# One core, a decoder trunk with experts: the results of each small expert item are scattered by the next small item

## The reference

```
def moe_swiglu(h, router, w_gate, w_up, w_down):
    tok = h.reshape(B * S, D)
    logits = (tok @ router).astype(jnp.float32)
    top_v, top_i = lax.top_k(logits, TOP_K_EXPERTS)
    w = jax.nn.softmax(top_v, axis=-1)
    gates = jnp.sum(jax.nn.one_hot(top_i, N_EXPERTS) * w[..., None], axis=1)
    out = jnp.zeros_like(tok)
    for e in range(N_EXPERTS):
        out = out + gates[:, e:e + 1] * swiglu(tok, w_gate[e], w_up[e], w_down[e])
    return out
```

## Time and profile before

| | |
|---|---|
| median of 3 runs | 1305.22 us (1303.74 to 1307.96) |
| the profiled execution | 1304.98 us |
| its span, first to last instruction | 1303.2 us |
| mean granted TensorE clock | 0.99 |
| PE busy | 1242.6 us, 95% |
| DVE busy | 637.7 us, 49% |
| ACT busy | 568.5 us, 44% |
| POOL busy | 112.3 us, 9% |
| read from HBM | 422.23 MB |

### The profile page before, as it was taken

One profiled execution on the slowest core, in us unless ns is written; L12 is line 12 of the kernel. 1 busy time (PEld: TensorE's weight loads), 2 busy tenths in 40 slices (PEclk: granted clock), 3 DMA queues, 4 the chain that ended last, 5 costly groups with the idle time before them and its releaser, 6 DMA issues.

```text
span 1303.2 us, 18423 instructions
## 1 busy us (share of the span) xinstructions
PE 1242.6 (95%) x7254; PEld 880.2 (68%) x7254; DVE 637.7 (49%) x754; ACT 568.5 (44%) x871; POOL 112.3 (9%) x262
## 2 busy tenths in 40 slices
PE   9999999999999999899999989999989999998776
PEld 8988999999989833577853367774338777333222
DVE  6886755547755300588820078880028885000001
ACT  6665544435656300577720177761027775001002
POOL 1000000000000461100210100201010021001000
PEclk9999999999999899999999999999999999999999
DMA  9943554358432399999999999999999999999996
GB/s 332 356 152 115 184 195 162 130 174 279 171 143 78 129 401 418 404 415 415 408 369 415 417 408 415 421 383 391 416 409 412 414 416 359 417 419 402 415 416 256
DMA packets 116487, 424.47 MB, mean 326 GB/s; under 512 B 4625, under 2 KB 23218, under 8 KB 108594
## 3 DMA queue, kind: packets, MB, share of 16 engines
q1 hardware_dynamic: 116192, 422.75, 83.0%
q10 hardware_dynamic: 210, 0.54, 0.1%
HBM read 422.23 MB, written 1.05 MB: 325 GB/s over the span
## 4 chain that ended last, share of the span: by engine, by line
PE 79%; DMA 17%; DVE 2%; ACT 1%; issue 1%; SPq 0%; POOL 0%; POOLq 0%; ACTq 0%; DVEq 0%
DMA ring<-in_moe_w_down 8%; PE psA L1571 7%; PE psA L1573 7%; PE psA L1572 7%; PE psB L1571 7%; PE psB L1573 7%; PE psB L1572 7%; DMA ring<-in_moe_w_up 6%; PE psA L1955 5%; PE psB L1955 5%; PE psY L1571 5%; PE psY L1573 5%; PE psY L1572 5%; PE psY L1946 4%; DMA ring<-in_moe_w_gate 2%; PE psY L1719 1%
## 5 line engine op out<-in xcount | busy, mean ns | idle before, releaser
L1436 DVE TENSOR_TENSOR wlo<-ring,whi 128x2048 fp32r<-128x2048 f32 (+1 forms) x135 | 287.2, 2150 | 84.9 <-ACT whi L812 83.9
L812 ACT CAST whi<-ring 128x1024 fp32r<-128x1024 f32 x252 | 261.0, 1051 | 89.1 <-PE psA L1573 28.6
L1183 DVE TENSOR_TENSOR wlo<-ring,whi 128x1024 fp32r<-128x1024 f32 (+2 forms) x104 | 152.3, 1485 | 17.8 <-ACT whi L630 17.7
L630 ACT CAST whi<-ring 128x1024 fp32r<-128x1024 f32 (+1 forms) x134 | 133.4, 1023 | 59.3 <-PE psY L1573 28.2
L1946 PE MATMUL psY<-ring,squares_of 128*64 128x512 f32 x560 | 126.8, 596 | 7.3 <-DMA ring<-in_moe_w_down 7.1
L1515 DVE TENSOR_TENSOR hidT<-psB,hidT 128x512 f32<-128x512 f32 (+1 forms) x16 | 10.0, 625 | 243.4 <-PE psB L1955 177.4
L1955 PE MATMUL psB<-ring,resT 128*64 128x512 f32 x480 | 106.6, 594 | 8.9 <-DMA ring<-in_moe_w_up 8.8
L1955 PE MATMUL psA<-ring,resT 128*64 128x512 f32 x480 | 107.6, 596 | 5.6 <-DMA ring<-in_moe_w_gate 5.6
L1571 PE MATMUL psA<-xhi,whi 128*128 128x256 f32 x368 | 104.9, 285 | 2.6 <-DVE wlo L1183 1.2
L1571 PE MATMUL psB<-xhi,whi 128*128 128x256 f32 x368 | 106.4, 289 | 0.0
L1572 PE MATMUL psA<-xlo,whi 128*128 128x256 f32 x368 | 102.8, 279 | 0.0
(11 more groups left out here) (351 smaller groups left out, 2265.0 us busy)
## 6 DMA issues: line engine op xcount, KB each, us to landing
ring<-in_moe_w_gate SPq DMA_DIRECT2D x56, 2048.0 KB, 19.0
ring<-in_moe_w_up SPq DMA_DIRECT2D x56, 2048.0 KB, 20.4
ring<-in_moe_w_down SPq DMA_DIRECT2D x56, 2048.0 KB, 21.0
ring<-in_ffn_w_gate SPq DMA_DIRECT2D x5, 2048.0 KB, 9.1
ring<-in_ffn_w_up SPq DMA_DIRECT2D x5, 2048.0 KB, 7.9
ring<-in_ffn_w_down SPq DMA_DIRECT2D x5, 2048.0 KB, 8.0
ring<-in_moba_w_qkv SPq DMA_DIRECT2D x8, 1024.0 KB, 7.4
ring<-in_diff_w_qkv SPq DMA_DIRECT2D x6, 1024.0 KB, 12.2
```

The lines of the kernel that those rows point to most:

```text
L630: nc.scalar.copy(hi_of(m, size), part_of(ring, s, g, size)).then_inc(hi_done, size)
L812: nc.scalar.copy(hi_of(NG + m, 2), item_part(ring, j, g, 2)).then_inc(hi_done, 2)
L1183: nc.vector.tensor_tensor(part_of(wlo, s, g, size), part_of(ring, s, g, size), f(hi_of(m, size)), ALU.subtract).then_inc(lo_done, size)
L1436: nc.vector.tensor_tensor(item_part(wlo, j, g, step), item_part(ring, j, g, step), f(hi_of(NG + m, step)), ALU.subtract).then_inc(lo_done, ...
```

## The change

The big items scatter nothing. The small items 2, 4 and 6 scatter two results each: that of the small item two places ahead (parts 0, 1 ahead of slot gate 3, parts 2, 3 ahead of slot up 3) and then that of the big item just ahead (ahead of slots gate 5 and up 5). The result of a small item waits in its buffer through the big item. The loop (item 7) scatters as before, at gate 3 and gate 5. The waits on `scatter_mm` and `add_done` are counted anew with `scattered(i)`, and each pair of scatter matmuls now waits for the adds of the pair before it.

```diff
-    SCATTER_AT = {item_slot["gate", 3, 2, 0]: (0, 2), item_slot["gate", 5, 2, 0]: (2, 4)}
+    SPREAD_AT = item_slot["gate", 5, 2, 0]
+    SCATTER_AT = [item_slot[kind, c, 2, 0] for c in (3, 5) for kind in ("gate", "up")]
@@
+        def scatters(i):
+            if not isinstance(i, int) or i >= LAST:
+                return {SCATTER_AT[0]: (i - 1, 0, 2), SCATTER_AT[2]: (i - 1, 2, 4)}
+            if not i or i in BIG_AT:
+                return {}
+            return {SCATTER_AT[a]: (i - 2 + a // 2, a % 2 * 2, a % 2 * 2 + 2) for a in range(4)}
+
+        def scattered(i):
+            return 4 * (i - 1 if isinstance(i, int) and i in BIG_AT else i)
@@ ACT, result
-                if not isinstance(i, int) or i:
-                    act.wait_ge(scatter_mm, 4 * i)
+                if not isinstance(i, int) or i >= 2:
+                    act.wait_ge(scatter_mm, scattered(i))
@@ DVE, few_rows
-                    if n in (1, 2):
-                        add_rows(i - 1, 2 * n - 2, 2 * n)
+                    for at, what in scatters(i).items():
+                        if n in (1, 2) and (at < SPREAD_AT) == (n == 1):
+                            add_rows(*what)
@@ DVE, expert
-                    if j in SCATTER_AT:
-                        add_rows(i - 1, *SCATTER_AT[j])
@@ PE, gather_rows
-                    if not isinstance(i, int) or i >= 2:
-                        pe.wait_ge(add_done, 4 * (i - 1))
+                    if not isinstance(i, int) or i >= 3:
+                        pe.wait_ge(add_done, scattered(i - 1))
@@ PE, scatter
-                if first:
+                if first or not isinstance(i, int) or i:
                     pe.wait_ge(add_done, 4 * i + first)
@@ PE, expert
-                    if j in SCATTER_AT:
-                        scatter(i - 1, *SCATTER_AT[j])
@@ PE, few_rows
-                    if j in SCATTER_AT:
-                        if not isinstance(i, int) or i:
-                            scatter(i - 1, *SCATTER_AT[j])
-                        elif SCATTER_AT[j][0]:
-                            spread_T()
+                    if j in scatters(i):
+                        scatter(*scatters(i)[j])
+                    if isinstance(i, int) and i == 0 and j == SPREAD_AT:
+                        spread_T()
```

## The result

| | before | after |
|---|---|---|
| median of 6 runs each | 1305.33 us (1300.12 to 1307.96) | 1294.04 us (1291.71 to 1297.49) |
| profiled execution | 1304.98 us | 1297.49 us |
| its span | 1303.2 us | 1295.7 us |
| PE busy | 1242.6 us | 1240.2 us |
| POOL busy | 112.3 us | 100.5 us |

The ratio is 0.9921, 95% interval 0.9898 to 0.9943: faster by 10.3 us by the ratio, and 11.3 us between the medians. Between the two profiled executions lie only 7.5 us, near the forecast of 6.4. The rest of this text is about both differences: what the 7.5 us are, and where 3 to 4 more come from.

What follows compares the result with a forecast made beforehand. The prediction took a DMA weight stream with three PE-made gaps at the big items' ends as the bound. Removing 2.12 us from each of three big items, 6.4 us, gave 1304.98 - 6.4 = 1298.6 us; range 1295.5 to 1303.0.

Steps and rivals of the forecast that it cites:

- What bounds the kernel: Whole expert part: DMA stream at some 413 GB/s, with three PE-made gaps of 3.3 to 3.8 us, one per big item.
- The sum: Whole kernel: 1304.98 - 6.4 = 1298.6 us, with all other parts of the change taken as worth nothing.
- the term of the removed pairs: Big items, PE: two scatter pairs of 1.06 us removed from each of three items, all regained as DMA time, 6.4 us.
- rival 1: Heads of items 3 and 5: full clock comes back too, giving 1297.0 us, or 1295.8 with both items; chance 0.22.
- The base: Starting time: the profiled execution, 1304.98 us, lies 0.24 us below the median, so no correction.
- The small items: Items 2, 4, 6: added pairs at 1.2 us each, 2.4 us an item, covered by 6.3 and 5.33 us of PE idle time.
- DVE, POOL and the new waits: Moved adds, `spread` writes, selection and added waits in big and small items: all cost or gain nothing.
- POOL's chain: Selection for item 3, ended 7.4 us after the scatter; moves into item 2, some 28 us ahead of the gather; costs nothing.
- Rival 2: Gaps at the big items' ends: slowest of 16 DMA engines goes on as before, half regained, 1301.8 us; chance 0.12.
- rival 3: Whole kernel: no change, 1305.0 us, as the DMA stream is untouched and gaps are not PE's or reappear elsewhere; chance 0.09.

Runs made afterwards that it cites:

- e6: Kernel before, with each pair of scatter matmuls in the big items made twice: 1310.11 us, ratio 1.0028.
- e5: Kernel before, with 36 useless transposes in PE's idle time ahead of each big item: 1298.92 us, ratio 0.995.
- e4: Changed kernel, with 36 useless transposes in PE's idle time ahead of each big item: 1295.81 us.
- e9: Kernel before, with twelve useless transposes in PE's short waits of the routing: 1301.54 us, ratio 0.9983.
- e8: Changed kernel, with three useless 128-row matmuls ahead of each of four scatter slots in small items 2, 4 and 6: 1306.99 us.
- e12: Kernel before, with two useless pairs of 64-row matmuls in each of small items 2, 4, 6 and twelve transposes in the routing: 1301.70 us.
- e10: Changed kernel, with twelve useless transposes in PE's short waits of the routing: 1292.86 us, ratio 0.9911.
- e1: Changed kernel measured again, unedited: 1293.74 us, ratio 0.9924.
- e2: Changed kernel, with the older result's scatter in small items 2, 4 and 6 only 8 columns wide instead of 512: 1297.02 us.
- e7: e4 with twelve more useless transposes in PE's short waits of the routing: 1291.90 us, ratio 0.9895.

## Why the prediction was wrong, point by point

**What bounds the kernel: right.** Three gaps at the ends of the big items, each made by PE, a DMA stream at full rate elsewhere. The shorter the big item, the higher the rate in the three windows: from 341 GB/s in e6 over 354 before, 386 in e5 and 398 after to 407 in e4 (means; set by the ends of the big items, over 50 us, they are 379, 387, 401, 409 and 412).

**The sum: the term of the removed pairs was too small.** It stood at 3 x 2 x 1.06 = 6.4 us. The pair is worth 1.24 us (1.23 at gate 3), since the step from the turn to the pair (0.53 us) is longer than the step from the turn to the product (0.35 us): 7.4 us. I measured the pair from its own start and did not bound what its absence does to its neighbour. Measured from head to head: 7.7 and 7.8 us. What is over 7.4 is not shown apart; the clock is the likely part. Item 5 had 6.8 us at half clock in the profile before, 5.6 of it in work; after, the stretch is 3.4 us, and the item got 3.5 us shorter where items 1 and 3 got 2.5. That is part of rival 1, though hardly for its reason: idle time ahead of item 5 fell by 0.7 us only, and e9 shows both lengths at idle times of 5.0 to 5.1 us.

**The base: the step that failed most.** "It lies 0.24 us below the median, so no correction is made." The profiled execution had the routing at half clock, and the median lay beside it in the upper group; 1300.12 came only with the later executions. Over all runs the executions of the kernel before lie from 1299.4 to 1308.0, most of them below 1303 or above 1304.7; those of the changed kernel at 1291.7 to 1295.6 and at 1297.3 to 1297.5. The median before came from the upper group, that after from the lower: two executions of twelve of the changed kernel lie in its upper group, of the kernel before four of 6 in the result above. With the routing still the two medians are 8.7 us apart instead of 11.3. The term of the pairs at its measured 7.4 us would have given 1297.6 us, and even 8.7 us below the median of 1305.3 would be 1296.6, both inside the range. What put the result below 1295.5 are the other 2.6 us, by these runs most likely the draw of executions with and without half clock in the routing. My range had no term for this, although the three times shown spread over 4.2 us. Whether the change itself makes the lower group likelier is open: e4 and e8, which have it too, have four of 6 (1295.4 to 1296.3, the others at 1291) and eight of 12 (1305.9 to 1309.7, the others at 1302.7) in their upper groups, which speaks for chance. The profiles in the last paragraph on e9 to e12 leave the same question open for the heads of the big items.

**The small items: right in sign, too dear.** I had 2.4 us of added work and 3.9 and 2.9 us of idle time left; it is 4.48 and 4.67. The pairs cost 1.06 us each, not 1.2, and part of them went into waits inside the small item: in item 2 PE had waited 1.33 us for `w_down` and 0.61 us ahead of the gather, and after the change it waits for neither. The cover holds, and e8 shows where it ends. Predicted heads of items 3 and 5: 755.3 and 969.7; found: 754.16 and 969.15.

**DVE, POOL and the new waits: right.** No wait of PE for `spread` or for adds shows in the small items after, and the selection written in item 2 is in time. The 7.4 us that I took for POOL's chain from the earlier trace rows came to 3.5 us (698.99 to 702.45), since the same copy of `rel_now` and the selection behind it are shorter there. Before, in big item 1, and after, in small item 2:

```profile
619.45 2.25 POOL L1119 COPY rel_now<-rel 128x4 f32<-128x4 f32 x1
```

```profile
699.67 0.19 POOL L1130 COPY rel_now<-rel 128x4 f32<-128x4 f32 x1
700.10 2.35 POOL L1136 TENSOR_SCALAR equal<-slotno,rel_now 128x128 f32<-128x128 f32 x4
```

DVE was busy for 7.33 of 9 us around the first (618 to 627) and for 1.13 of 4 us around the second (699 to 703); that this is the cause was not tested. Over all items the copy and the selection took 12.0 us less, which is the 11.8 us by which POOL's busy time fell; none of it is on the path.

**The rivals.** Rival 2 (half) and 3 (none) fall with e6 and e10; with rival 3 falls the reading that only the most-contended engine counts (the Trainium skill, Perfetto Trace Analysis, Identifying Performance Opportunities, where the quoted sentence stands). The Trainium skill (Perfetto Trace Analysis, Optimization Strategy) says to find the gaps on the engine that one optimizes for and what it waits for there. The trace agrees: with two pairs out of PE's way the first gap went from 355 to 395 GB/s. Rival 1's lower bound of 1295.8 was too high since its 6.4 us were.

## What to carry to other kernels

In a stream that is bound by DMA for most of the time, look at its rate in windows of 20 to 30 us: a dip says where another engine may hold the stream back, and doubling that engine's suspected work there (e6) shows whether it does. Moving 2.5 us of such work to where the same engine idles was worth the whole 2.5 us here, until the dip was filled. Price a removed instruction from the end of the one ahead to the start of the one behind, with a row of the same neighbours without it if there is one. Before a forecast of half a per cent, ask whether the profile has a stretch, anywhere, whose clock could differ from one execution to the next.

## What the runs showed of the hardware

The granted clock of one piece of code differs between executions. In the routing, PE's waits of 0.26 to 0.39 us between short matmuls were followed by 10.2 us (before), 6.8 us (e1) or nothing (e2) at half clock, worth up to 5 us. With twelve transposes in the waits the clock was 1.00 in all five profiles (e7, e9 to e12); without them it was 1.00 in three of nine (e2, e5, e6). Ahead of the big items, 5.0 to 5.1 us of idle time went with 3.4 or 6.8 us at half clock, also in one execution and for one code. In e9, around the heads of items 1, 3 and 5 (in the last two the clock fell before the first matmul):

```profile
535.30:538.70 3.40, 3.40 (x8) 2.72 (x9) 3.40 (x7) 2.38 (x3) 0.00 (x0) 0.50 1.03 411
538.70:542.10 3.40, 3.40 (x16) 2.72 (x16) 3.40 (x4) 2.42 (x3) 0.00 (x0) 1.00 1.02 406
750.30:757.10 6.80, 4.17 (x10) 3.31 (x11) 6.51 (x8) 5.61 (x7) 0.00 (x0) 0.50 1.03 404
968.80:975.60 6.80, 5.80 (x14) 4.55 (x15) 6.80 (x10) 4.18 (x5) 0.00 (x0) 0.50 1.04 411
```

The changed kernel's windows at the heads of items 3 and 5:

```profile
754.20:757.60 3.40, 3.40 (x8) 2.72 (x9) 3.40 (x7) 2.29 (x3) 0.00 (x0) 0.50 1.03 410
969.20:972.60 3.40, 3.40 (x8) 2.71 (x9) 3.40 (x7) 2.47 (x3) 0.00 (x0) 0.51 1.02 408
```

Eight matmuls in 3.40 us, where 0.233 us each gives 14.6. With 1.0 to 1.1 us of idle time left ahead of the big items (e4, e5, e7) the clock stayed at 1.00 there. The same POOL copy took 2.25 us in a stretch with DVE busy for 7.33 of 9 us and 0.19 us in one with DVE busy for 1.13 of 4. A 2 MB load landed 7.6 to 9.8 us after its issue at the end of item 1, in the gap, and 28.3 us after it in the saturated stream.
